# Turning U's tiles on VectorE: moved out of the query stage and the ring, with a third buffer for K's pages

## The reference, cut to what matters

```
h  = rms(x) * (1 + sc1) + sh1
z  = h @ w_in                       # three branches and three gates
a  = HGRN2 recurrence               # 4 heads of 128
b  = forgetting attention           # 8 heads of 64; samples read paged K, V, log forget
c  = gated DeltaNet                 # 4 heads of 128
x += g1 * (sum_i sigmoid(gate_i) * (o_i @ w_br_i)) @ w_out
h2 = rms(x) * (1 + sc2) + sh2
q  = h2 @ w_q                       # 8 heads, scores against 2 x 128 sub-keys
top 16 of each half, 256 sums, top 16, softmax -> 16 experts of 16384 per head
x += g2 * sum_e g_e * gelu(u_e . h2) * v_e
```

## Time and profile before

| | |
|---|---|
| median of 3 runs | 5140.17 us (5133.6 to 5150.63) |
| the profiled execution's own time | 5153.22 us |
| its span, first to last instruction | 5151.6 us |
| mean granted TensorE clock | 0.962 |
| busy: TensorE, VectorE, POOL, ScalarE | 93%, 57%, 36%, 21% of the span |
| bytes that the DMA queues moved | 1501.92 MB, mean 292 GB/s |
| turns L1528: count, busy, wait for u_rows | 240 + 16 out of the ring; 1.24 us each; 254 us |

### The profile page before, as it was taken

How to read it: one execution, slowest core, us unless ns; L and a number is a source line. 1 busy time by engine, 2 the same in 40 slices (tenths; PEclk the granted TensorE clock), 3 DMA queues, 4 the chain that set the end, 5 groups by cost and what they waited for, 6 DMA issues and landing times.

```text
span 5151.6 us, 84355 instructions
## 1 busy us (share of the span) xinstructions
PE 4809.7 (93%) x25236; PEld 3797.1 (74%) x25236; DVE 2920.3 (57%) x5723; ACT 1069.0 (21%) x2652; POOL 1865.8 (36%) x2629
## 2 busy tenths in 40 slices
PE   8999989889989999999989998898889899989998
PEld 6887777567777776777768877765678777767776
DVE  3653331424789788666636433324247897876665
ACT  1112111211111577000011121112101115770000
POOL 4531100123554444444345321001245444444543
PEclk8999999889999999999999999998899999999999
DMA  8763689477789999999977537795778899999998
GB/s 292 261 206 117 187 252 305 143 258 251 261 317 361 348 363 338 386 415 410 377 276 269 188 111 221 227 315 159 252 249 283 310 363 349 361 328 408 414 409 324
DMA packets 726936, 1501.92 MB, mean 292 GB/s; under 512 B 64976, under 2 KB 405968, under 8 KB 725024
## 3 DMA queue, kind: packets, MB, share of 16 engines
q0 software_dynamic: 253344, 870.76, 45.6%
q1 hardware_dynamic: 473216, 626.61, 36.1%
HBM read 1328.58 MB, written 302.75 MB: 317 GB/s over the span
## 4 chain that ended last, share of the span: by engine, by line
PE 71%; issue 8%; DMA 7%; DVE 6%; SPq 3%; DVEq 2%; POOL 1%; POOLq 1%; ACT 1%; ACTq 0%
PE PS L1379 19%; PE PS L1322 16%; PE PS L819 8%; PE PS L715 7%; PE PS L1254 3%; PE PS L946 3%; DMA u_rows<-arena 2%; PE PS L1334 2%; DMA ring<-in_wst 1%; SPq L507 1%; DMA xT<-u_rows,arena 1%; PE PS L750 1%; PE PS L738 1%; DVE arena L1528 1%; PE PS L1148 1%
## 5 line engine op out<-in xcount | busy, mean ns | idle before, releaser
L1322 PE MATMUL PS<-hT,ring 128*128 128x288 f32 x4096 | 1018.5, 407 | 27.9 <-DMA ring<-in_uv 27.9
L1379 PE MATMUL PS<-arena,ring 128*128 128x288 f32 x4096 | 994.5, 406 | 0.8 <-DMA ring<-in_uv 0.8
L1322 PEld LDWEIGHTS PS<-hT,ring 128*128 128x128 f32 x4096 | 771.9, 191 | 232.6 <-issue 28.8
L1379 PEld LDWEIGHTS PS<-arena,ring 128*128 128x128 f32 x4096 | 777.9, 190 | 217.1 <-DMA ring<-in_uv 1.7
L819 PE MATMUL PS<-hT,ring 128*128 128x272 f32 x2304 | 605.6, 409 | 8.5 <-DMA ring<-in_wst 8.5
L580 POOL DMA_DIRECT2D u_rows<-arena x1024 | 568.6, 556 | 113.3 <-issue 27.6
L1992 DVE SCALAR_TENSOR_TENSOR PS<-xT,arena,PS 128x1024 f32<-128x1024 f32 x368 | 474.4, 1289 | 226.7 <-DMA xT<-v_rows,arena 214.0
L694 POOL DMA_INDIRECT xT<-u_rows,arena x410 | 404.4, 986 | 498.1 <-DVE arena L1983 378.6
L2219 ACT ACTIVATE arena<-PS 128x272 f32<-128x272 f32 (+21 forms) x570 | 218.3, 393 | 1517.5 <-PE PS L819 544.5
L1983 DVE CUSTOM_DVE_ANT_0 xT<-xT,PS 128x1024 f32<-128x1024 f32 x410 | 494.3, 1216 | 56.7 <-DMA xT<-u_rows,arena 50.4
L819 PEld LDWEIGHTS PS<-hT,ring 128*128 128x128 f32 x2304 | 439.0, 198 | 102.1 <-issue 19.3
(11 more groups left out here) (415 smaller groups left out, 5629.8 us busy)
## 6 DMA issues: line engine op xcount, KB each, us to landing
ring<-in_uv SPq DMA_DIRECT2D x512, 512.0 KB
ring<-in_wst SPq DMA_DIRECT2D x312, 512.0 KB
u_rows<-arena POOLq DMA_DIRECT2D x1024, 128.0 KB, 4.7
v_rows<-in_uv SPq DMA_DIRECT2D x256, 512.0 KB, 6.5
arena<-in_uv POOLq DMA_DIRECT2D x240, 512.0 KB, 6.0
arena<-in_ck SPq DMA_DIRECT2D x128, 256.0 KB, 5.0
arena<-in_cvv POOLq DMA_DIRECT2D x64, 256.0 KB, 4.6
gate_tiles<-arena SPq DMA_DIRECT2D x96, 136.0 KB, 4.7
```

What stands on the lines that cost most here:

```text
L1322: i = mm(PS[:, 2 + s % 2, 0:TD], ring[:, s, c, :], hD[:, c, :], start=(c == 0), stop=(c == DC - 1))
L1379: i = mm(PS[:, 2 + b, 0:TD], ring[:, s, j, :], WB[:, row, :], start=(row == 0), stop=(row == NK - 1))
```

## The change

- 8 tiles are no longer turned out of the ring (N_U3 = 0). All 128 have their own load, so the ring's tiles of U wait for nothing but their slots.
- 20 tiles (N_UX) are turned between the HGRN2 states and the second chunk of the gated DeltaNet, in xT's room, with two input and two output buffers there. For this, x is copied to DRAM (`x_kept`) after the first norm and copied back when the paged attention is done, ahead of the merge's first U loads in POOL's queue. POOL's 72 log-forget DMAs now stand behind these 20 tiles.
- The merge turns 18 tiles instead of 6, the output projection 24 instead of 18 (3 behind each residual), the query stage 6 instead of 36.
- K's pages have a third buffer, in xT's room (q = 2 and 5): the load for q waits for scores q-3.
- The routes are wanted earlier and the one-hots begin earlier: I_RT = 64, I_OH = 65, N_EARLY = 112; so 63 groups lie in the U pass and 9 after it.

```diff
-N_U1, N_U2, N_U3 = 60, 60, 8
-U_FIRST, U_AT_OUT = 18, N_U1 + 24
+N_U1, N_UX, N_U2, N_U3 = 60, 20, 48, 0
+N_L = N_U1 + N_UX + N_U2
+U_MERGE, U_OUT = 18, 24
+U_FIRST, U_AT_OUT = 18, N_U1 + N_UX + U_MERGE + U_OUT
...
-N_EARLY = 108
+N_EARLY = 112
-I_RT, I_OH = 68, 69
+I_RT, I_OH = 64, 65
...
+    k_room = lambda q: xflat[:, 0:4096] if q % 3 == 2 else AR[:, 12 * T + (q % 3) * 4096:12 * T + (q % 3 + 1) * 4096]
...
             for q in range(NSEQ):
-                if q >= 2:
-                    sp.wait_ge(qs_mm.sem, qs_mm.at(l, q - 1))
+                if q == 2:
+                    for m in (N_U1 + N_UX - 2, N_U1 + N_UX - 1):
+                        sp.wait_ge(us_st[m % 3].sem, us_st[m % 3].at(l, 64 * (m // 3 + 1)))
+                        sp.nop(nofuse=True)
+                if q >= 3:
+                    sp.wait_ge(qs_mm.sem, qs_mm.at(l, q - 2))
...
+        def u_tiles_in_x(l):
+
+            def step(m, k, load):
+                g.wait_ge(ut_v.sem, l * NK + k * 6 + (m + 1))
+                g.nop(nofuse=True)
+                if load:
+                    u_load(l, k * 6 + (u_tile(m) + 2), m + 2)
+                u_store(k * 6 + u_tile(m), m)
...
+            g.wait_ge(h_r.sem, h_r.at(l, 1))
+            g.nop(nofuse=True)
+            g.dma_start(xkept, xflat).then_inc(xk_st.sem, 16)
...
+            g.wait_ge(xk_st.sem, xk_st.at(l, 16))
+            g.nop(nofuse=True)
+            u_tiles_in_x(l)
             g.wait_ge(rw_g.sem, rw_g.at(l, 1))
...
             g.wait_ge(qt_mm.sem, qt_mm.at(l, 8))
             g.nop(nofuse=True)
-            u_tiles(l, N_U1, N_U1 + N_U2)
+            g.dma_start(xflat, xkept).then_inc(xr_ld.sem, 16)
+            u_tiles(l, N_U1 + N_UX, N_L)
...
             headnorm(l, 0)
             tt(Qs, Qs, GAs, ALU.mult)
             v.drain().then_inc(oa_r.sem, 1)
+            turn_in_x()
...
             v.drain().then_inc(rw_g.sem, 1)
-            headnorm(l, 1)
+            turn_in_x(2)
+            headnorm(l, 1, turn_in_x)
...
                 tt(v3(W[8]), m3(ident[:, :]), v3(W[4]), ALU.subtract)
                 v.drain().then_inc(g_v.sem, 1)
+                turn_in_x()
...
                 tt(Wn(8), bk(0), Wn(8), ALU.add)
                 v.drain().then_inc(g_v.sem, 1)
+                turn_in_x()
...
                     cp(Wn(5), bk(5)).then_inc(g_v.sem, 1)
+                    turn_in_x()
...
                 v.drain().then_inc(gk_r.sem, 1)
+                turn_in_x(2)
...
                 for c4 in range(4):
-                    if c4 < 3:
-                        turn_u(N_U1 + c4, kc)
+                    for m in range(c4 * 9 // 4, (c4 + 1) * 9 // 4):
+                        turn_u(N_U1 + N_UX + m, kc * 3)
...
-                    for m in range(s * 9 // 4, (s + 1) * 9 // 4):
-                        turn_u(N_U1 + 6 + m, k * 3)
+                    for m in range(3 * s, 3 * s + 3):
+                        turn_u(N_U1 + N_UX + U_MERGE + m, k * 4)
```

More of the change, by code:

```diff
@@ L393, in build @@
     pt_ld = Sig("page_table_loaded", 16)
-    lg_ld, ln_ld, lg_r = Sig("past_logf_loaded", 16 * 64), Sig("new_logf_loaded", 16 * 8), Sig("past_forget_ready", 1)
-    kc_ld = [Sig("k_pages_loaded0", 16 * 32), Sig("k_pages_loaded1", 16 * 32)]
+    lg_ld, lg_r = Sig("logf_loaded", 16 * 72), Sig("past_forget_ready", 1)
+    kc_ld = [Sig(f"k_pages_loaded{b}", 16 * 8 * len(range(b, NSEQ, 3))) for b in range(3)]
     vc_ld = [Sig("v_pages_loaded0", 16 * 32), Sig("v_pages_loaded1", 16 * 24), Sig("v_pages_loaded_ring", 16 * 8)]
@@ L409, in build @@
     vn_ld = Sig("v_rows_laid", 16 * NK)
-    ul_ld = [Sig(f"u_tile_loaded{b}", 16 * (N_U1 + N_U2) // 3) for b in range(3)]
+    ul_ld = [Sig(f"u_tile_loaded{b}", 16 * len(range(b, N_L, 3))) for b in range(3)]
     ut_v = Sig("u_tile_turned", NK)
@@ L580, in u_store @@
                 g.dma_start(ulaid[i, q], u_out(m)[32 * q:32 * q + 32, :].rearrange("p (e n) -> p e n", e=4)).then_inc(us_st[m % 3].sem, 16)
+        def u_tiles_in_x(l):
[5 more added lines that the diff above has]
+                u_store(k * 6 + u_tile(m), m)
+            for m in (N_U1, N_U1 + 1):
+                u_load(l, u_tile(m), m)
+            with g.Fori(0, N_UX // 6) as k:
+                for b in range(6):
+                    step(N_U1 + b, k, True)
+            for m in (N_U1 + N_UX - 2, N_U1 + N_UX - 1):
+                step(m, 0, False)
         def u_tiles(l, m0, m1):
@@ L667, in _ @@
             g.dma_start(xkept, xflat).then_inc(xk_st.sem, 16)
-            for m in range(N_U1 + N_U2, NK):
+            for m in range(N_L, NK):
                 g.wait_ge(ut_v.sem, ut_v.at(l, m + 1))
@@ L1487, in norm_query, with headnorm @@
             v.drain()
-        def headnorm(l, g):
+        def headnorm(l, g, behind=lambda: None):
             v.wait_ge(hn_rt.sem, hn_rt.at(l, g + 1))
@@ L1493, in headnorm @@
             v.drain().then_inc(hn_rc.sem, 1)
+            behind()
             for n, (slot, _, _, _, gain) in enumerate(HN[g]):
@@ L1515, in turn_u @@
             def turn_u(m, k=0):
-                n = m - N_U1 - N_U2
+                n = m - N_L
                 if n < 0:
@@ L1524, in turn_u, with turn_in_x @@
                 v.nop(nofuse=True)
-                if m >= 3:
-                    v.wait_ge(us_st[m % 3].sem, k * 64 + us_st[m % 3].at(l, 64 * (m // 3)))
+                last = m - 2 if N_U1 + 2 <= m < N_U1 + N_UX else m - 3
+                if last >= 0:
+                    v.wait_ge(us_st[last % 3].sem, k * 64 + us_st[last % 3].at(l, 64 * (last // 3 + 1)))
                     v.nop(nofuse=True)
                 NV.transpose(u_out(m).rearrange("p (e c b) -> p e c b", e=4, c=DC), src).then_inc(ut_v.sem, 1)
+            in_x = iter(range(N_U1, N_U1 + N_UX))
+            def turn_in_x(n=1):
+                for m in itertools.islice(in_x, n):
+                    turn_u(m)
             norm_scale(l)
@@ L1952, in _ @@
             v.drain()
+            v.wait_ge(xr_ld.sem, xr_ld.at(l, 16))
+            v.nop(nofuse=True)
             with v.Fori(0, 2) as k:
@@ L2043, in head_best @@
                 rows_ = [(n, 2 * h + e) for n in range(4) for e in range(2)] if h < 8 else [(4, j) for j in range(4)]
-                later = iter(range(U_AT_OUT + (N_U2 - 24) * h // 8, U_AT_OUT + (N_U2 - 24) * (h + 1) // 8) if h < 8 else ())
+                later = iter(range(U_AT_OUT + (N_U2 - U_MERGE - U_OUT) * h // 8, U_AT_OUT + (N_U2 - U_MERGE - U_OUT) * (h + 1) // 8) if h < 8 else ())
                 calls = itertools.count()
```

38 lines of the change are left out of this document (23 added, 15 removed).

## The result

The median is **5104.45 us** (5093.0 to 5108.5) against 5140.17 before: ratio **0.9922**, 95% interval 0.9903 to 0.9942. The profiled execution took 5094.1 us, span 5092.4. I forecast 5142 and "no change"; what came is at the bottom of the range, and clear of noise where I had forecast no change. In number it is my rival B (5106). In mechanism it is B only in part, as "Why the prediction was wrong" shows. The time differs by a few us from session to session: the kernel before, measured again beside the experiments, had medians of 5144.9, 5144.9 and 5144.1, so kernels of different sessions are best compared by their ratios.

What follows compares the result with a forecast made beforehand. TensorE was taken to bound most of the time, with the stages taking over turns near or at the DMA limit. Terms -27.9 - 18.7 - 22 + 39 + 18 + 8 + 5 = +1.4 gave 5142 us against the median 5140.2; range 5104 to 5172.

Steps and rivals of the forecast that it cites:

- rival B: Whole kernel: the DMA gives way more easily, K's waits vanish, merge costs 4 us a layer: 5106 us; chance 0.33.
- U pass, start: Start of the U pass: TensorE's stall for the ring goes and no new wait for routes appears: -27.9 us.
- One-hots: Behind the U pass: eight groups a layer move into it, 3.48 us saved and 1.14 paid for each: -18.7 us.
- K's third room: Paged attention's sequences: a third K buffer saves 11 us a layer, nearer to one block's load than all waits: -22 us.
- Output projection: Output projection: six more turns a layer at 3.63 us, TensorE waiting for them at the norm: +39 us.
- Merge: Merge: twelve more tiles and x's copy make 104 us of DMA work in 90, 9 us a layer: +18 us.
- x's room: Delta chunks 0 and 1: twenty turns' transfers overfill the DMA engines, 4 us a layer, bounds 1 and 15: +8 us.
- V pass: V pass: VectorE gets four more rows, 2.5 us a layer later after its slack: +5 us.
- Nothing, as forecast: x's copy to DRAM and 16 extra tile loads lie in stages with room: 0, at most 2 us.
- Rival C: Delta chunks 0 and 1: TensorE waits for late ring loads, 15 us a layer, merge at 14: 5174 us; chance 0.24.
- D: U pass: the stall only moves, late routes or ring tile cost 12 us a layer again: 5166 us; chance 0.03.

Runs made afterwards that it cites:

- routes68: The changed kernel with routes asked for at tile 68 and one-hots from tile 69, four groups a layer back behind the U pass: 5129.1 us, ratio 0.9974.
- k_two_rooms: The changed kernel, K's three buffers kept, but the load of sequence q waits for the scores of q-2, as with two: 5133.2 us, ratio 0.9985.
- out_small: The changed kernel with the 24 tiles a layer for the output projection's turns loading 64 of their 1024 columns: 5099.7 us, ratio 0.9912.
- x_small: The changed kernel with the twenty tiles turned in xT's room loading 64 of their 1024 columns; turns, stores and waits stay: 5103.3 us, ratio 0.9924.
- 60 / 20 / 18 / 12 / 18: Turns a layer in z stage, xT's room, merge, output projection, query stage; against the changed kernel twelve moved from output projection to query stage: 5060.3 us, ratio 0.9834.
- merge30: The changed kernel with 30 turns a layer in the merge, 12 in the output projection, 6 in the query stage: 5143.5 us, ratio 0.9996.

## Why the prediction was wrong

The sum was +1.4, the profiles say -59, of which 15 are the delta and fox stretches' spread: -44 to explain, and the medians say -36. By its items, both layers together:

1. **U pass, start** (-27.9): right, and too small. From its start to its ninth tile the pass takes 46.9 and 48.4 us before and 31.1 twice after: -33.1. The missing 5 us go with the granted clock, 0.85 in the 19 us behind the stall against 1.00 after. The routes kept their slack: the sum of the weights begins at 4209.71 and TensorE asks at 4222.45, 12.7 us as before.
2. **One-hots** (-18.7): the tail was right (27.8 forecast, 26.6 found). The term +9.1 for eight groups in the pass was mis-sized: after the stall is taken out, the pass is 4 us shorter, and routes68 shows no price either. Why less idle time lies between the groups is not shown. I had charged the groups the whole difference between the pass's pitch and a bare tile.
3. **K's third room** (-22): the mechanism held, k_two_rooms shows it, at -30. I held it near "one block less" because the DMA engines seemed nearly full (share 0.94), and I priced the waits only, without the clock that a wait takes from the matmuls behind it.
4. **Output projection** (+39): right, +43 with the norm. The term's cause was left between two readings, bytes (2.9) or pace (3.63); out_small decides for the pace, and its trace points at GpSimd's issuing. The reciprocal comes 188.0 us after the merge's start (3820.99 - 3633.0) instead of 167, 21 later and not 29, since the merge adds nothing.
5. **Merge** (+18): **the step that failed most.** "104 us of DMA work in 90" added up busy shares. The stage took in all its bytes in the same 92.1 us, for 0 instead of +9 a layer: 0.98 x 92 of engine time for 373 GB/s in the first layer's merge, where 0.68 had carried 227. By the share before, 373 GB/s would have wanted 1.12. The share that a stretch shows at part load is no measure of what its bytes need. What bounds the merge once the turns are many is VectorE's chain of turns, which I had priced in item 4 and not looked for here: at 18 turns it fits with a little to spare, at 30 it costs 43 us a layer. The Trainium skill ("DMA: Bandwidth & Descriptors", Anatomy of one DMA) gives 436 GB/s for the bytes of a transfer beside its fixed 2 us; the prediction's estimate from the bytes alone, 98 us for the merge, was nearer but would have charged it too.
6. **x's room** (+8): the same step, the same error. The 64 us of work in 58 came as 357 GB/s at a share of 1.07. What it cost was about 1 us a layer by TensorE's idle time in chunks 0 and 1 (x_small): my lower bound, not my 4.
7. **V pass** (+5): right, +7.6. TensorE's last wait shows it (L1421, 3.9 a layer), and routes68 gives 4.1 and 4.8 back.
8. Nothing, as forecast.

With the merge at 0, x's room at 2, the groups in the pass at 0 and K at its measured 30, the same working gives -27.9 - 27.8 - 30 + 39 + 2 + 5 = -40. That is an account after the fact and no forecast. Rival B, to which I gave 0.33, had the direction and the thought behind it right, that the DMA gives way. That its 5106 is so near is in part luck: it still charged the merge 8 us and the groups 9, had K's waits vanish (half of them stayed, and the clock made up for it), and left out the clock at the U pass. Rival C is refuted: the ring's waits in the delta chunks (L854) did not grow, 6.9 us against 8.5. So is D: TensorE starts the U pass without a gap. The forecast's largest price was also the one worth avoiding: six turns fewer behind the residuals give 35 us and twelve 44, so the kernel with 60 / 20 / 18 / 12 / 18 is at 5060.

## What to carry to other kernels

Busy shares of DMA engines don't add: before charging a transfer to a stage, divide the bytes that the stage will have by the highest rate that any stretch of the same profile reached. That gives a least time and no more: for merge30 it gave at most 25 us more a layer, and 43 came. A chain of turn, issue and landing has a pace of its own. Look which link is busy nearly all of the time (here GpSimd, by its waits), count how many rounds fit beside TensorE's work, and put the rest where the engines have room, down to the idle time that the profile shows. When a wait is removed, add the matmuls behind it that ran at the lower clock.

## What the runs showed of the hardware

- **A wait costs TensorE twice.** 24 K matmuls take 1.99 us at a granted clock of 1.00 (2.4 GHz), and 3.75 us at 0.50 (1.2 GHz) behind a wait of 5.22 us. With shorter waits the granted clock of the whole stage went from 0.76 to 0.83, and TensorE's busy time in it fell by 9 us. The Trainium skill ("Perfetto Trace Analysis", Matmul Optimizations) says that the engine scales its power with its utilisation, so that matmuls should come back to back in batches; the trace agrees in so far as the granted clock fell behind the waits, with these numbers.
- **Full DMA engines have no one rate.** At shares of 0.96 to 1.07 the stretches of after moved 314, 335, 357, 373 and 380 GB/s. TensorE had no wait for the ring in the merge and the output projection, and 1.2 us at most in a layer's chunks 0 and 1.
- **GpSimd's issue is a resource.** 0.55 us for each transfer and 0.62 from start to start: five for a tile make at least 3.3 us of the 3.6 us pace, which neither fewer bytes nor landings shorter by 2 to 3 us moved (out_small: 3.57). A store in one transfer instead of four was not tried, so how much of the pace it would give is open.
